# Experts of 704-column chunks: silu, product, turns and parts one to three units later, and a silu at the head of the loop

## The chip, the cores and the metric

The kernel runs on one core of a Trainium2 chip. The metric is the device time of one launch in microseconds (us). The kernel before takes 2733.32 us, the median of 3 runs (2729.62 to 2734.46).

## What is computed

Two groups of tokens (128 prompt, 512 sample; 640 together, model width 1024) go through a trunk of two layers. The second layer ends in a mixture of experts, and that stage is the one of this case. Its reference, cut to what matters:

```python
def swiglu(x, w_gu, w_dn):
    g, u = jnp.split(x @ w_gu, 2, axis=-1)
    return (jax.nn.silu(g) * u) @ w_dn

def moe_swiglu(h, router_w, router_b, w_gu, w_dn):
    ...
    _, idx = lax.top_k(logits + router_b.astype(jnp.float32), TOP_K)      # 2 of 8 experts
    ...
    for ex in range(N_EXPERTS):
        y = y + gates[:, ex:ex + 1] * swiglu(xf, w_gu[ex], w_dn[ex])      # 1024 -> 2 x 1408 -> 1024
```

## The kernel before

The expert stage is the loop of `tail_stage` over 17 tiles (`SLOT_TILES`) of 128 token slots each. A tile belongs to one expert. Every engine has its own loop over the tiles and, in it, its own row of 27 units (`NU`), written out by hand; semaphores tie the rows together.

- **Units.** A unit is one piece of weights. Units 0 to 3 are the gate weights of the first chunk of 704 columns (`ECH`), 4 to 7 its up weights, 8 to 11 and 12 to 15 the same for the second chunk (1408 columns to a partition each), and 16 to 26 are the eleven row blocks of the down weights (1024 columns to a partition each).
- **SyncE** (L3065 to L3076) loads unit u into a ring of 9 raw buffers, when VectorE has finished with unit u - 9.
- **ScalarE** (L3243 to L3266) copies unit u into `m_hi` (L3248, rounded to the fast float format), when TensorE has finished unit u - 9. Behind certain units it also does: the copy of the last tile's result (`AT_Y`, unit 4), the silu of a chunk's gates (`AT_SILU`, units 7 and 15), the high parts of the turned activations (`part_a`, `AT_PART_A`, units 14, 15, 21, 22), and the high parts of the next tile's turned rows (`part_x`, `AT_PART_X`, unit 19).
- **VectorE** (L3386 to L3400) makes `m_lo`, the rest of unit u (L3389), and behind certain units the product silu x up (`AT_ACT`, units 11 and 19, L3394), and the low parts belonging to the same `part_a` and `part_x` (L3378, L3373).
- **TensorE** (L3149 to L3196) multiplies unit u when `m_lo` of it is there: 12 matmuls of 352 columns for a gate or up unit (L3166 to L3169), 6 of 512 columns for a down unit (L3182 to L3186). Between units it transposes: `turn_a` c (L3134) turns part c of the 1408 activations, in the four parts of 2, 3, 3 and 3 blocks of 128 columns (`TA`), and `turn_x` (L3127) the rows gathered for the next tile (8 blocks, behind unit 16). The turns alternate between two banks of `p_turned`; a turn waits until VectorE has emptied its bank (L3138), and `turn_a` also for the product of its chunk (L3137).
- **Down units and parts.** Down unit k is unit 16 + k. Before k = 0, 2, 5 and 8 TensorE waits until VectorE has finished the low part of turn 0, 1, 2 or 3 (L3176 to L3178). So unit 21 (k = 5) waits for the parts of `turn_a` 2, and unit 24 (k = 8) for those of `turn_a` 3.
- **Other waits of TensorE.** Unit 8 waits for the first silu (L3156), unit 12 for the first product (L3159). Unit 0 of the next tile waits for the second silu and for the parts of the next rows (L3148).
- **Function tables.** ScalarE needs a table of functions in place. A load of one (ACT_TABLE_LOAD) is put in by the compiler ahead of an activation whose function is not in the table that it knows to be there. In this loop there is one ahead of the first copy of a tile (L3248) and one ahead of the first silu (L3261).

Of the kernel before, what the change touches and what calls it, by code (L numbers as in the profile page):

```python
# [18 lines left out]
ACT = mybir.ActivationFunctionType  # L19
# [6 lines left out]
P = 128  # L26
# [30 lines left out]
ECH = 2 * 352  # L57
# [2893 lines left out]
def tail_stage(K, z, flip, expert_of):  # L2951
# [9 lines left out]
    NTURN = len(TA) + 2  # L2961
    X_USES, A_USES = (2, 3), (0, 1, 4, 5)

    AT_Y, AT_SILU, AT_ACT, AT_PART_A, AT_PART_X = 4, (7, 15), (11, 19), (14, 15, 21, 22), 19
    assert NU % MRAW == 0 and NU % MSPLIT == 0
    ks = range(J // 2)
    tokens = [lambda j, t, h=h: h[:, j, t * P:(t + 1) * P] for h in (K.h_hi, K.h_lo)]
# [35 lines left out]
    with ExitStack() as ctx:  # L3003
        raw = K.sb(ctx, "m_raw", [P, MRAW, MUNIT])
        xg = K.sb(ctx, "x_gathered", [P, D])
        xh, xl = K.sb(ctx, "x_hi", [P, J, P], F32R), K.sb(ctx, "x_lo", [P, J, P], F32R)
        silu = K.sb(ctx, "m_silu", [P, ECH])
        act = K.sb(ctx, "m_act", [P, D_EXPERT])
        ah, al = K.sb(ctx, "m_a_hi", [P, DN, P], F32R), K.sb(ctx, "m_a_lo", [P, DN, P], F32R)
        ysb = K.sb(ctx, "y_slot", [P, D])  # L3010
        whi, wlo = K.sb(ctx, "m_hi", [P, MSPLIT, MUNIT], F32R), K.sb(ctx, "m_lo", [P, MSPLIT, MUNIT], F32R)
        idx = K.sb(ctx, "slot_tokens", [P, SLOT_TILES + 1], I32)

        K.sb(ctx, "gap", [P, 1000 - ECH // 2])
        tok, idx0 = K.sb(ctx, "token_ids", [P, NT], I32), K.sb(ctx, "first_tokens", [P, 1], I32)
        zero = K.sb(ctx, "slot_zero", [P, SLOTS // P], I32)
        pG, pU = K.ps(ctx, "p_gates", [P, 2, 512]), K.ps(ctx, "p_ups", [P, 2, 512])
        pT, pD = K.ps(ctx, "p_turned", [P, 2, 512]), K.ps(ctx, "p_down", [P, 2, 512])
        landed = [K.sig(f"m_landed{s}") for s in range(MRAW)]
        names = ("hi", "lo", "used", "silu", "act", "turned", "t_hi", "t_lo", "y")  # L3020
        s_hi, s_lo, s_used, s_silu, s_act, s_turned, s_thi, s_tlo, s_y = (K.sig("m_" + n) for n in names)
        s_clear = K.sig("m_cleared")
        s_stored, s_idx, s_gather = K.sig("m_stored"), K.sig("m_slots", own=True), K.sig("m_gathered", own=True)
        wgu = I["moe_w_gu"][0].rearrange("e (p j) (h n) -> e p j h n", j=J, h=2)
        wdn = I["moe_w_dn"][0].rearrange("e (j p) n -> e p j n", p=P)

        def gu(ring, u):
            return ring[:, u % ring.shape[1], :].rearrange("p (j q n) -> p j q n", j=2, q=2)

        def chunk_of(u):  # L3030
            c, r = divmod(u, 2 * KU)
            return c, *divmod(r, KU)

        def size(u):
            return MUNIT if u < GU else D


    def use(tile, j):
        return NTURN * tile + (2 + j)

    with nc.Block() as block:
# [38 lines left out]
        def _(pe):  # L3080
# [53 lines left out]
            def turn_a(tile, c):  # L3134
                a, b = TA[c]

                pe.wait_ge(s_act.sem, s_act.at(tile * CH + (c // 2 + 1)))  # L3137
                pe.wait_ge(s_tlo.sem, s_tlo.at(use(tile, A_USES[c]) - 1))  # L3138
                for j in range(a, b):
                    mm = pe.transpose(pT[:, A_USES[c] % 2, (j - a) * P:(j - a + 1) * P], act[:, j * P:(j + 1) * P], K.ident[:])  # L3140
                mm.then_inc(s_turned.sem, 1)
# [4 lines left out]
            with pe.Fori(0, SLOT_TILES) as tile:  # L3146

                pe.wait_ge(s_tlo.sem, s_tlo.at(NTURN * tile + 2))  # L3148
                for u in range(NU):  # L3149
                    s = u % MSPLIT  # L3150
                    if u < GU:
                        c, half, k = chunk_of(u)
                        acc = (pG, pU)[half]
                        if k == 0 and half == 0:

                            pe.wait_ge(s_silu.sem, s_silu.at(tile * CH + c))  # L3156
                        elif k == 0:

                            pe.wait_ge(s_act.sem, s_act.at(tile * CH + c))  # L3159
                        pe.wait_ge(s_lo.sem, s_lo.at(tile * NU + (u + 1)))  # L3160
                        h, l = gu(whi, u), gu(wlo, u)
                        for b in range(2):
                            j = 2 * k + b
                            start, stop = j == 0, j == J - 1
                            for q in range(2):
                                pe.matmul(acc[:, q, 0:ECH // 2], xh[:, j, :], h[:, b, q, :], start=start, stop=False)  # L3166
                                pe.matmul(acc[:, q, 0:ECH // 2], xh[:, j, :], l[:, b, q, :], start=False, stop=False)  # L3167
                            for q in range(2):
                                mm = pe.matmul(acc[:, q, 0:ECH // 2], xl[:, j, :], h[:, b, q, :], start=False, stop=stop)  # L3169
                        mm.then_inc(s_used.sem, 1)  # L3170
                    else:
                        k = u - GU
                        if k == 0:

                            pe.wait_ge(s_y.sem, s_y.at(tile + 1))
                        for c in range(len(TA)):  # L3176
                            if k == TA[c][0]:
                                pe.wait_ge(s_tlo.sem, s_tlo.at(use(tile, A_USES[c]) + 1))  # L3178
                        pe.wait_ge(s_lo.sem, s_lo.at(tile * NU + (u + 1)))
                        for half in range(2):  # L3180
                            cs = slice(half * 512, half * 512 + 512)
                            pe.matmul(pD[:, half, :], ah[:, k, :], whi[:, s, cs], start=k == 0, stop=False)  # L3182
                            pe.matmul(pD[:, half, :], ah[:, k, :], wlo[:, s, cs], start=False, stop=False)  # L3183
                        for half in range(2):
                            cs = slice(half * 512, half * 512 + 512)
                            mm = pe.matmul(pD[:, half, :], al[:, k, :], whi[:, s, cs], start=False, stop=k == DN - 1)  # L3186
                        mm.then_inc(s_used.sem, 1)
                    if u in (10, 11):
                        turn_a(tile, u - 10)
                    if u == 16:  # L3190

                        pe.wait_ge(s_gather.sem, s_gather.at(tile * 16 + 32))
                        for half in range(2):
                            turn_x(use(tile, X_USES[half]), half)
                    if u in (19, 20):
                        turn_a(tile, u - 17)  # L3196


        @block.scalar
        def _(a):  # L3200
# [39 lines left out]
                part_x(half, half, half)  # L3240
            a.wait_ge(s_clear.sem, s_clear.at(1))
            with a.Fori(0, SLOT_TILES) as tile:
                for u in range(NU):  # L3243
                    s = u % MRAW
                    a.wait_ge(landed[s].sem, landed[s].at((tile * (NU // MRAW) + (u // MRAW + 1)) * 32))

                    a.wait_ge(s_used.sem, s_used.at(tile * NU + (u - MSPLIT + 1)))
                    a.activation(whi[:, u % MSPLIT, 0:size(u)], raw[:, s, 0:size(u)], ACT.Copy).then_inc(s_hi.sem, 1)  # L3248
                    if u == AT_Y:

                        a.wait_ge(s_used.sem, s_used.at(tile * NU))
                        a.wait_ge(s_stored.sem, s_stored.at(tile * 16))
                        a.activation(ysb[:], pD[:].rearrange("p h n -> p (h n)"), ACT.Copy).then_inc(s_y.sem, 1)  # L3253
                        a.wait_ge(s_y.sem, s_y.at(tile + 1))
                        a.dma_start(K.y_slots[bass.ds(tile * P, P), :], ysb[:]).then_inc(s_stored.sem, 16)
                    if u in AT_SILU:
                        c = AT_SILU.index(u)
                        a.wait_ge(s_used.sem, s_used.at(tile * NU + (2 * KU * c + KU)))

                        a.wait_ge(s_act.sem, s_act.at(tile * CH + c))  # L3260
                        a.activation(silu[:].rearrange("p (q n) -> p q n", q=2), pG[:, :, 0:ECH // 2], ACT.Silu).then_inc(s_silu.sem, 1)  # L3261
                    if u in AT_PART_A:
                        part_a(tile, AT_PART_A.index(u))
                    if u == AT_PART_X:
                        for half in range(2):
                            part_x(use(tile, X_USES[half]), half, half)  # L3266
# [372 lines left out]
```

## Time and profile before

| what | value |
|---|---|
| median of 3 runs | 2733.32 us |
| the profiled execution: its time, its span | 2734.22 us, 2732.4 us |
| TensorE (PE) busy over the span | 2493.9 us, 91% |
| VectorE (DVE), ScalarE (ACT), GpSimd (POOL) busy | 59%, 51%, 15% |
| the expert loop, from the first weights copied to the last result | 1853 to 2688 us |
| time from one tile to the next in it | 48.74 us |

A matmul is pipelined, so the busy time of PE counts overlapping spans; what a unit costs is read as the distance from its first matmul to that of the next unit. PE stands for the matmuls and PEld for the weight loads of TensorE. In the timeline, neighbouring instructions of the same kind are merged to one row with their count, and square brackets hold the idle time of the engine ahead of the row and what ended it.

### The profile page before, as it was taken

The numbers are of one execution on the slowest core, as the hardware profiler recorded it, in microseconds if no ns is written. First come the engines' busy times: TensorE is split into PE (matmuls) and PEld (weight loads), VectorE is DVE, ScalarE is ACT, GpSimd is POOL, SyncE is SP. The second block draws the span as 40 slices with busy tenths as digits, with TensorE's granted clock in tenths as the row PEclk, the third lists the DMA queues.
The fourth block names the chain that finished last, engine by engine and source line by source line (L and its number), as shares of the span: only waits on it lengthen the run. The fifth ranks groups of instructions, "written<-read, shape, count | busy, mean of one in ns | idle before, by whom it ended". The sixth has DMA issues, their size and how long they took to land. (4 is left out here: it accounts for less than half of the span.)

```text
span 2732.4 us, 51986 instructions
## 1 busy us (share of the span) xinstructions
PE 2493.9 (91%) x19059; PEld 2159.2 (79%) x19059; DVE 1605.4 (59%) x2296; ACT 1386.4 (51%) x2083; POOL 397.5 (15%) x571
## 2 busy tenths in 40 slices
PE   6998969999789999899899788878999999999993
PEld 4887958778478888787677788767999989999892
DVE  3255566665753233223311688547888888888886
ACT  4235755554323333212222566417878788787883
POOL 1133122221141000011100343041000000000003
PEclk9999989999999999999899899978999999999997
DMA  7530000000541222223254000319999999999994
GB/s 270 202 126 3 18 5 3 3 3 3 205 147 47 77 77 69 77 77 127 98 191 145 31 19 10 119 69 356 382 370 380 383 367 384 368 378 386 366 386 188
DMA packets 193213, 472.23 MB, mean 173 GB/s; under 512 B 29436, under 2 KB 62844, under 8 KB 186916
## 3 DMA queue, kind: packets, MB, share of 16 engines
q1 hardware_dynamic: 185568, 445.69, 45.2%
q0 software_dynamic: 4416, 14.70, 1.5%
q10 hardware_dynamic: 3076, 9.71, 0.9%
q8 instruction: 108, 1.77, 0.3%
q14 instruction: 45, 0.37, 0.0%
HBM read 453.54 MB, written 16.48 MB: 172 GB/s over the span
## 5 line engine op out<-in xcount | busy, mean ns | idle before, releaser
L3389 DVE TENSOR_TENSOR m_lo<-m_raw,m_hi 128x1408 fp32r<-128x1408 f32 (+1 forms) x459 | 643.2, 1456 | 54.4 <-ACT m_hi L3248 49.3
L3248 ACT ACTIVATE m_hi<-m_raw 128x1408 fp32r<-128x1408 f32 (+1 forms) x459 | 537.5, 1241 | 15.5 <-ACT y_slot L3253 11.9
L213 PE MATMUL acc<-w_hi,h_hi 128*128 128x512 f32 (+1 forms) x1120 | 432.7, 386 | 17.2 <-PEq L2800 7.9
L195 DVE TENSOR_TENSOR w_lo<-w_raw,w_hi 128x1024 fp32r<-128x1024 f32 (+1 forms) x132 | 162.0, 1231 | 485.2 <-ACT w_hi L190 484.4
L214 PE MATMUL acc<-w_lo,h_hi 128*128 128x512 f32 (+1 forms) x1120 | 425.5, 380 | 0.0
L215 PE MATMUL acc<-w_hi,h_lo 128*128 128x512 f32 (+1 forms) x1120 | 425.5, 380 | 0.0
L190 ACT ACTIVATE w_hi<-w_raw 128x1024 fp32r<-128x1024 f32 (+1 forms) x134 | 135.1, 1012 | 456.8 <-PE acc L215 407.6
L213 PEld LDWEIGHTS acc<-w_hi,h_hi 128*128 128x128 f32 x1120 | 213.4, 191 | 79.7 <-issue 33.7
L215 PEld LDWEIGHTS acc<-w_hi,h_lo 128*128 128x128 f32 x1120 | 213.3, 190 | 34.6
L214 PEld LDWEIGHTS acc<-w_lo,h_hi 128*128 128x128 f32 x1120 | 213.7, 191 | 32.7
L3166 PE MATMUL p_gates<-m_hi,x_hi 128*128 128x352 f32 x544 | 179.3, 331 | 8.2 <-DVE m_lo L3389 8.2
L3167 PE MATMUL p_gates<-m_lo,x_hi 128*128 128x352 f32 x544 | 176.3, 325 | 0.0
L3166 PE MATMUL p_ups<-m_hi,x_hi 128*128 128x352 f32 x544 | 176.2, 325 | 0.0
L3167 PE MATMUL p_ups<-m_lo,x_hi 128*128 128x352 f32 x544 | 175.1, 323 | 0.0
L3182 PE MATMUL p_down<-m_hi,m_a_hi 128*128 128x512 f32 x374 | 152.7, 408 | 0.1
L3183 PE MATMUL p_down<-m_lo,m_a_hi 128*128 128x512 f32 x374 | 146.2, 391 | 0.0
L3169 PE MATMUL p_gates<-m_hi,x_lo 128*128 128x352 f32 x544 | 131.8, 323 | 0.0
L3169 PE MATMUL p_ups<-m_hi,x_lo 128*128 128x352 f32 x544 | 130.4, 320 | 0.0
L3422 POOL DMA_INDIRECT x_gathered<-scratch_h_rows,slot_tokens x17 | 17.0, 1002 | 743.7 <-PE p_turned L3131 737.1
L1232 POOL TENSOR_TENSOR x<-x,gated 128x512 f32<-128x512 f32 x30 | 46.9, 1586 | 535.2 <-DVE gated L1225 535.2
L3166 PEld LDWEIGHTS p_gates<-m_hi,x_hi 128*128 128x128 f32 x544 | 104.1, 191 | 15.3 <-DVE m_lo L3389 15.3
L3186 PE MATMUL p_down<-m_hi,m_a_lo 128*128 128x512 f32 x374 | 116.1, 392 | 0.0
(407 smaller groups left out, 4908.3 us busy)
## 6 DMA issues: line engine op xcount, KB each, us to landing
m_raw<-moe_w_gu SPq DMA_DIRECT2D x544, 352.0 KB
m_raw<-moe_w_dn SPq DMA_DIRECT2D x187, 512.0 KB
ada_w<-ada_w SPq DMA_DIRECT2D x40, 1024.0 KB, 4.9
w_raw<-ffn_w_gu SPq DMA_DIRECT2D x88, 256.0 KB, 2.9
w_raw<-w_in_o SPq DMA_DIRECT2D x24, 512.0 KB, 5.8
w_raw<-ffn_w_dn SPq DMA_DIRECT2D x22, 512.0 KB, 3.6
w_raw<-w_in_e SPq DMA_DIRECT2D x28, 384.0 KB, 5.2
scratch_y_slots<-y_slot ACTq DMA_DIRECT2D x18, 512.0 KB, 6.7
```

Source lines behind the costliest of these rows:

```text
L190: eng.activation(hi, self.raw_of(c, k), ACT.Copy).then_inc(self.hi.sem, 1)
L195: eng.tensor_tensor(lo, self.raw_of(c, k), hi, ALU.subtract).then_inc(self.lo.sem, 1)
L213: eng.matmul(out, hi, whi[:, b, :], start=first, stop=False)
L214: eng.matmul(out, hi, wlo[:, b, :], start=False, stop=False)
L215: mm = eng.matmul(out, lo, whi[:, b, :], start=False, stop=last)
L3166: pe.matmul(acc[:, q, 0:ECH // 2], xh[:, j, :], h[:, b, q, :], start=start, stop=False)
L3167: pe.matmul(acc[:, q, 0:ECH // 2], xh[:, j, :], l[:, b, q, :], start=False, stop=False)
L3169: mm = pe.matmul(acc[:, q, 0:ECH // 2], xl[:, j, :], h[:, b, q, :], start=False, stop=stop)
L3182: pe.matmul(pD[:, half, :], ah[:, k, :], whi[:, s, cs], start=k == 0, stop=False)
L3183: pe.matmul(pD[:, half, :], ah[:, k, :], wlo[:, s, cs], start=False, stop=False)
L3248: a.activation(whi[:, u % MSPLIT, 0:size(u)], raw[:, s, 0:size(u)], ACT.Copy).then_inc(s_hi.sem, 1)
L3389: dve.tensor_tensor(wlo[:, u % MSPLIT, 0:n], raw[:, u % MRAW, 0:n], whi[:, u % MSPLIT, 0:n], ALU.subtract).then_inc(s_lo.sem, 1)
```

## The change

Five things move, and one is added, all in the expert loop:

- the silu of a chunk's gates from behind units 7 and 15 to behind 8 and 16 (ScalarE);
- the product from behind units 11 and 19 to behind 13 and 21 (VectorE);
- `turn_a` 0 and 1 from behind units 10 and 11 to behind 12 and 13, and `turn_a` 2 and 3 from behind units 19 and 20 to both behind unit 20 (TensorE);
- the parts of the activations from behind units 14, 15, 21, 22 to behind 17, 18, 24, 25 (ScalarE and VectorE);
- the parts of the next rows from behind unit 19 to behind 22 (ScalarE and VectorE);
- a silu of one element per partition opens each pass of ScalarE's loop. Its result is not used. Its buffer is taken out of an unused gap, so that all others stay where they are.

```diff
-    AT_Y, AT_SILU, AT_ACT, AT_PART_A, AT_PART_X = 4, (7, 15), (11, 19), (14, 15, 21, 22), 19
+    AT_Y, AT_SILU, AT_ACT, AT_PART_A, AT_PART_X = 4, (8, 16), (13, 21), (17, 18, 24, 25), 22
...
-        K.sb(ctx, "gap", [P, 1000 - ECH // 2])
+        one = K.sb(ctx, "table_first", [P, 2])
+        K.sb(ctx, "gap", [P, 998 - ECH // 2])
...
-                    if u in (10, 11):
-                        turn_a(tile, u - 10)
+                    if u in (12, 13):
+                        turn_a(tile, u - 12)
...
-                    if u in (19, 20):
-                        turn_a(tile, u - 17)
+                    if u == 20:
+                        turn_a(tile, 2)
+                        turn_a(tile, 3)
...
             with a.Fori(0, SLOT_TILES) as tile:
+                a.activation(one[:, 1:2], K.ones[:, 0:1], ACT.Silu)
```

## Rows read from the trace of the kernel before

**Rows 1.** Busy time by stretch: us, PE, PEld, DVE, ACT, POOL (x), PEclk, DMA, GB/s.

```profile
2100.40:2149.10 48.70, 48.50 (x279) 44.92 (x278) 42.39 (x35) 38.74 (x39) 0.94 (x1) 1.00 0.99 377
```

**Rows 2.** Waits, 1850 to 2720 us: us in total, times, longest us.

```profile
PE p_gates L3166 <- DVE m_lo L3389: 8.2, 17, 5.0
...
PEld p_down L3182 <- DVE m_lo L3389: 7.5, 17, 0.5
...
ACT m_hi L3248 <- DMA m_raw<-moe_w_gu: 2.9, 3, 2.4
```

**Rows 3.** Timeline of PE, gate units: start us, us, instruction, count, idle before.

```profile
2202.18 0.32 PE L3166 MATMUL p_gates<-m_hi,x_hi 128*128 128x352 f32 x1
...
2204.10 0.32 PE L3166 MATMUL p_gates<-m_hi,x_hi 128*128 128x352 f32 x1
```

**Rows 4.** Timeline of PE, turns and down units, into the next tile.

```profile
2232.93 1.05 PE L3131 MATMUL p_turned<-ident,x_gathered 128*128 128x128 f32 x8
...
2237.94 0.49 PE L3140 MATMUL p_turned<-ident,m_act 128*128 128x128 f32 x3
...
2239.66 0.49 PE L3140 MATMUL p_turned<-ident,m_act 128*128 128x128 f32 x3
2239.90 0.48 PE L3182 MATMUL p_down<-m_hi,m_a_hi 128*128 128x512 f32 x1
...
2241.39 0.40 PE L3182 MATMUL p_down<-m_hi,m_a_hi 128*128 128x512 f32 x1
...
2244.44 0.39 PE L3182 MATMUL p_down<-m_hi,m_a_hi 128*128 128x512 f32 x1
...
2247.16 0.39 PE L3182 MATMUL p_down<-m_hi,m_a_hi 128*128 128x512 f32 x1
...
2248.87 0.43 PE L3166 MATMUL p_gates<-m_hi,x_hi 128*128 128x352 f32 x1 [0.19 <-DVE m_lo L3389]
...
2250.91 0.32 PE L3166 MATMUL p_gates<-m_hi,x_hi 128*128 128x352 f32 x1
```

**Rows 5.** Timeline of ACT, the same tile.

```profile
2209.04 1.28 ACT L3261 ACT_TABLE_LOAD   x1
...
2233.57 1.09 ACT L3232 ACTIVATE x_hi<-p_turned 128x512 fp32r<-128x512 f32 x2 [4.83 <-PE p_turned L3131]
...
2238.46 0.49 ACT L3237 ACTIVATE m_a_hi<-p_turned 128x384 fp32r<-128x384 f32 x1 [1.92 <-PE p_turned L3140]
2238.85 1.05 ACT L3248 ACTIVATE m_hi<-m_raw 128x1024 fp32r<-128x1024 f32 x1
...
2240.57 3.89 ACT L3248 ACTIVATE m_hi<-m_raw 128x1024 fp32r<-128x1024 f32 x4
2244.48 1.28 ACT L3248 ACT_TABLE_LOAD   x1
2245.78 6.45 ACT L3248 ACTIVATE m_hi<-m_raw 128x1408 fp32r<-128x1408 f32 x5
```

**Rows 6.** Timeline of DVE, the same tile.

```profile
2238.99 0.56 DVE L3378 TENSOR_TENSOR m_a_lo<-p_turned,m_a_hi 128x384 fp32r<-128x384 f32 x1 [0.99 <-ACT m_a_hi L3237]
...
2247.19 6.23 DVE L3389 TENSOR_TENSOR m_lo<-m_raw,m_hi 128x1408 fp32r<-128x1408 f32 x4 [0.90 <-ACT m_hi L3248]
```

**Rows 7.** Groups, 850 to 1150 us: busy us, mean ns | idle before, releaser.

```profile
L213 PE MATMUL acc<-w_hi,h_hi 128*128 128x512 f32 x398 | 155.7, 391 | 0.0
...
L190 ACT ACT_TABLE_LOAD x9 | 11.5, 1283 | 0.2
```

**Rows 8.** Timeline of ACT ahead of the loop: a small activation.

```profile
1841.27 0.21 ACT L3228 ACTIVATE choice_logits<-choice_logits 128x10 f32<-128x10 f32 x1 [15.04 <-DVE choice_logits L3361]
```

**Rows 9.** Stretches at 130 and 712 us, columns as in rows 1.

```profile
130.00:230.00 100.00, 93.45 (x594) 83.06 (x592) 52.65 (x69) 29.89 (x60) 31.51 (x22) 1.00 0.30 101
...
712.00:715.40 3.40, 3.18 (x9) 1.74 (x8) 0.82 (x1) 1.94 (x3) 1.21 (x1) 0.50 1.01 419
```

**Rows 10.** Waits of PE, 130 to 230 us.

```profile
PE shift_bank L988 <- ACT x L1042: 5.3, 4, 1.3
```

## The prediction

> **What bounds the kernel now.** I read the busy time by stretch first, then the waits of the expert loop, then the timelines of one tile, engine by engine. In a stretch as long as one tile TensorE is busy for 48.50 of 48.70 us at a granted clock of 1.00, while ScalarE has 10 us and VectorE 6 us of idle time [rows 1]. So TensorE sets the pace, and the other two and the loads have only to be in time. The loads are: DMA is at 377 GB/s with a share of 0.99 [rows 1], but ScalarE waited for a landing three times, 2.9 us in all [rows 2]. They have little to spare, and the change moves no more bytes.
>
> What TensorE loses is small. A gate or up unit takes 1.92 us from its first matmul to the next unit's [rows 3], a down unit 1.36 us (two of them 2.72, from 2244.44 to 2247.16) [rows 4]. All that is more than that in a tile is turns, a slower start behind each of them, and two waits for VectorE's low parts. One is at the head of the tile: in all 17 tiles the first gate unit waited for `m_lo`, 8.2 us in total, 5.0 of it once, so 0.2 us each in the others [rows 2]. The other is within the down units (7.5 us in 17 waits of the weight loads, 0.44 each) [rows 2]: units 22 and 23 took 3.05 us instead of 2.72 [rows 4]. Both come from the same thing. ScalarE is bound to TensorE's turns: the part of turn 2 stands behind its copy of unit 21, that of turn 3 behind 22, and it idles for 1.92 us until TensorE is done with unit 19 and turns [rows 5]. From there it has only a few copies' lead, and a table load of 1.28 us lies ahead of the next tile's first copy [rows 5].
>
> **The change, part by part.** I count from the end of unit 19, where turn 2 begins before (2237.94) [rows 4].
>
> *The head of the tile: a gain.* From the first matmul of unit 26 (2247.16) to that of unit 0 (2248.87) are 1.71 us, and from there to unit 1 (2250.91) 2.04 us [rows 4]. Undisturbed they are 1.36 and 1.92. So 0.35 + 0.12 = 0.47 us per tile can go, in 16 passages. Does the jump of the loop itself cost TensorE something? In the feed-forward loop, which passes its head nine times in a stretch (ScalarE's nine table loads there), TensorE's idle time is 0.0 [rows 7]; so I take nothing, with 0.1 us per passage as the other bound.
>
> *Turn 2 behind unit 20: a loss.* Before, turn 2 had unit 20 between itself and unit 21, which needs its parts. The path is: first transpose 2237.94, ScalarE's part starts at 2238.46 (0.52 later) [rows 4, 5], VectorE's low part at 2238.99 (0.53 later) and lasts 0.56 [rows 6]. It ended at 2239.55, and unit 21 began at 2239.90: covered by 0.35 us. After the change nothing stands between: unit 20, turn 2, turn 3, unit 21. The three transposes of turn 3 cover only their own length. From the first transpose to unit 21 I get 0.52 + 0.53 + 0.56 + 0.05 for the release = 1.66 us, where the two turns alone would take 0.49. That is a new wait of about 1.2 us in each tile, and all of TensorE's later work is queued behind it.
>
> The sum from the end of unit 19 to the start of unit 26: before 9.22 us (2237.94 to 2247.16) [rows 4]. After: unit 20 1.36 (no turn ahead of it now), the path 1.66, the slow start of unit 21 0.13 (it took 1.49, 2239.90 to 2241.39 [rows 4]), units 21 to 25 6.80: 9.95 us. So +0.73 us in each of 17 tiles. The gain of the wait at unit 23 and of one break less is already in it.
>
> *Are ScalarE and VectorE there when turn 2 is done?* It begins at 2239.30 on the clock of that tile (2237.94 + 1.36). ScalarE must be through copy 24: it idled 4.83 us ahead of the parts of the next rows [rows 5], and the three copies 20 to 22, at 0.97 us (3.89 for four [rows 5]), fit there; behind these parts (2234.66) copies 23 and 24 end by 2236.6. VectorE has the product and three low parts more ahead of the next rows' parts, by my count until 2236.5, and is through low part 24 by 2238.8; it is needed at 2240.4. So the 1.66 us stand alone.
>
> *Is the wait at the head really gone?* From turn 2's start: ScalarE's part begins at 0.52 and takes 0.39 (2238.46 to 2238.85 [rows 5]), copy 25 ends at 1.9, the part of turn 3 at 2.3, copy 26 at 3.2, table load and small silu at 4.7, copy 0 at 6.1 (6.45 for five [rows 5]), VectorE's low part 0 (6.23 for four [rows 6]) at 7.7. TensorE comes to unit 0 at 1.66 + 0.13 + 6 x 1.36 = 9.95. Spare: 2.2 us. Unit 23's low part was done before the turn.
>
> *The table load and the small silu.* Loads stand ahead of the first copy and of the first silu [rows 5], 1.28 us each. A silu at the head brings silu's table, and copies run on it already (no load ahead of those behind the first silu), so one load per tile goes. The small silu costs some 0.2 us (0.21 for a 10-element activation [rows 8]). That is 1.1 us of ScalarE per tile, at no gain in time: the head has its 2.2 us without it. In the first tile TensorE does wait for ScalarE, and 0.2 us are added once. The Trainium skill (ScalarE: Activation LUTs, What ACT_TABLE_LOAD costs) puts a change of set at about 2.66 us, as a drain of 1.38 us is added to the load. Here the four copies end at 2244.46, the load starts at 2244.48 and the next copy at 2245.78 [rows 5], so the rows show no drain. By the page the spare time at the head would be 0.8 us instead of 2.2, and the sum the same.
>
> *The other moves, at nothing.* Silu behind copy 8: TensorE needs it for unit 8, whose low part VectorE makes at the same time and for longer (1.6 us against 0.8). Product behind low part 13: unit 12 waits for it, so VectorE must now be two low parts and a product ahead at unit 12. It comes to the gates with the 2.2 us from the head in hand, wins 0.36 us per unit on TensorE (1.56 against 1.92), and the load of 1.28 us ahead of the silu is gone: cover about 4 us for a product of 0.9. Turns 0 and 1 cost the same two breaks. Unit 16 needs the part of turn 0, now behind copy 17: turn 0 is done two units before. The ring of nine copies allows a lead of eight units and the moves need five. SyncE's loads are issued when low parts are done, for units 20 to 24 earlier than before; no landing gets later.
>
> **The sum:** 17 x 0.73 = 12.4, less 16 x 0.47 = 7.5, plus 0.2: +5.1 us. The profiled execution took 2734.22 us, so 2739.3. It lies 0.9 above the median of the runs, on which I put the same 5.1: 2738.4 us, or 0.19% more. A measurement of this kernel tells about 0.2% (5.5 us) from no change, so this lies just inside.
>
> **The rivals.**
> - *Slower beyond doubt: the head keeps its wait.* If ScalarE or VectorE comes to the head over 2.2 us later than counted (say VectorE is behind at turn 2, since its low part 24 has 1.6 us to spare), the loss stays and the gain doesn't come: 12.4 + 0.2 gives 2745.9. For it: VectorE is busy for 42.4 of 48.7 us [rows 1]. Against: the idle times above. 8%.
> - *Not slower: the path of turn 2 is shorter than I read.* Its place is unit 21. It breaks even at 1.38 us instead of 1.66; hidden wholly, it would give -0.43 us and -0.47 us per tile, about 2718. It would need ScalarE to be released sooner by transposes that follow. Against it: in the turn of the next rows four more transposes follow the first four (2232.93), and ScalarE starts 0.64 later (2233.57) [rows 4, 5], the same delay behind the last of four as in turn 2 behind the last of three. 4%.
> - *The clock falls.* A wait of 1.2 us in each tile might make the granted clock fall from 2.4 to 1.2 GHz. It was 0.50 for the 3.4 us from 712.0 [rows 9]; one such step per tile costs 1.7 us, 29 in all: 2767. The rule behind it is in the Trainium skill (TensorE: Matmul & The Clock Gate, HAM oscillation), that a loop with a wait in each pass can fall back each time. Against it: between 130 and 230 us TensorE waited 1.3 us four times, 5.3 in all [rows 10], and the clock stayed at 1.00 [rows 9]. 3%.
> - *The compiler keeps the load at the silu.* ScalarE then has 1.3 us less between units 7 and 8, of about 4 to spare: the time of the forecast.
>
> **How the numbers follow.** The forecast of 2738.4 has 85%, with its own range of 2735 to 2742: the runs of before lie 4.8 us apart, the head's jump may cost up to 1.6, and the path is read to 0.1 us per tile. The range of 2732 to 2746 takes in the first rival and leaves out 2718 and 2767. Slower by over 0.2% (above 2738.8): 0.42 of the forecast's 85%, and the first and third rival, 0.47. Faster by over 0.2%: 0.04. Within: 0.49.
>
> **What would show it.** In the profile after: a wait of PE at the down units for VectorE's `m_a_lo` (L3378), 17 times at about 1.2 us; no wait of `p_gates` for `m_lo` but in the first tile; none at `p_down` for `m_lo`; 48.98 us from tile to tile; one table load per tile instead of two; ScalarE idle ahead of the second silu instead of ahead of the next rows. It is wrong if the waits at unit 21 are over 1.4 or under 0.9 us, if unit 12 waits for the product, or if ScalarE begins to wait for landings.

## The result, and the profile after

The kernel after takes 2740.73 us, the median of 9 runs (2738.39 to 2742.32), beside 2733.79 for the kernel before in 9 runs on the same chip (2728.47 to 2736.43). The ratio is 1.0028, with a 95% interval of 1.0017 to 1.0038. So the change is a small loss of 0.28%, or 6.9 us, and it stands clear of the scatter. The profiled execution took 2741.29 us; its span is the first line of the page:

```profile
span 2739.5 us, 52003 instructions
...
PE 2489.6 (91%) x19059; PEld 2164.9 (79%) x19059; DVE 1604.1 (59%) x2296; ACT 1366.2 (50%) x2083; POOL 401.1 (15%) x571
```

Nothing in this table of busy times tells of a loss. ScalarE even fell from 51% to 50%, because it loads half as many tables. The loss is in the waits. Here they are for the kernel after, from 1850 us on (us in total, times, longest us), and they answer to [rows 2]:

```profile
ACT m_silu L3264 <- PE p_gates L3170: 72.7, 17, 4.8
...
PEld p_down L3183 <- issue: 19.6, 17, 1.2
PE p_down L3183 <- DVE m_a_lo L3381: 15.7, 17, 0.9
...
ACT m_hi L3251 <- DMA m_raw<-moe_w_gu: 8.2, 13, 2.9
...
PE p_gates L3167 <- issue: 5.1, 1, 5.1
```

The wait at the head of the tile is left in the first tile alone (5.1 us, once), and the one of the down units for `m_lo` is gone. In their place stands one wait for `m_a_lo` in each of the 17 tiles. The view puts the part after the last transpose down to it, 0.92 us each; the weight load ahead of that matmul stood still for 1.15 us (19.6 / 17), which is nearly the whole gap of 1.17 (1.74 less the 0.57 that six transposes take up to the next matmul, as seen below).

The timeline of PE in the kernel after, one tile and the start of the next (start us, us, instruction, count, idle before), answers to [rows 4]:

```profile
2242.45 0.82 PE L3141 MATMUL p_turned<-ident,m_act 128*128 128x128 f32 x6
...
2288.81 0.39 PE L3183 MATMUL p_down<-m_hi,m_a_hi 128*128 128x512 f32 x1
...
2290.17 0.39 PE L3183 MATMUL p_down<-m_hi,m_a_hi 128*128 128x512 f32 x1
...
2291.53 0.82 PE L3141 MATMUL p_turned<-ident,m_act 128*128 128x128 f32 x6
2293.27 0.49 PE L3183 MATMUL p_down<-m_hi,m_a_hi 128*128 128x512 f32 x1 [0.92 <-DVE m_a_lo L3381]
...
2294.75 0.39 PE L3183 MATMUL p_down<-m_hi,m_a_hi 128*128 128x512 f32 x1
...
2300.19 0.39 PE L3183 MATMUL p_down<-m_hi,m_a_hi 128*128 128x512 f32 x1
...
2301.55 0.32 PE L3167 MATMUL p_gates<-m_hi,x_hi 128*128 128x352 f32 x1
...
2303.47 0.32 PE L3167 MATMUL p_gates<-m_hi,x_hi 128*128 128x352 f32 x1
```

Read as distances from start to start. From turn to turn: 2291.53 - 2242.45 = 49.08 us, one tile (49.06 to 49.08 from the second tile on, 48.72 to 48.74 before). Unit 20 takes 1.36 (2290.17 to 2291.53). The turns and the wait take 1.74 (to 2293.27) and unit 21 takes 1.48. From there to unit 26 (2300.19) there are 5.44 us, four undisturbed units of 1.36. Then come 1.36 to the first gate unit and 1.92 to the second, where before there were 1.71 and 2.04 [rows 4].

Where the 7.1 us between the two profiled executions came from:

| stretch | before | after | difference |
|---|---|---|---|
| launch to the first matmul of the loop | 1856.17 | 1857.26 | +1.1 |
| that matmul to the last result copy (2687.31; 2694.29) | 831.14 | 837.03 | +5.9 |
| from there to the end of the span | 45.1 | 45.2 | +0.1 |

Within the loop, the stretch from the end of unit 19 to the start of unit 26 is 10.02 us (2290.17 to 2300.19) against 9.22 before, and the passage of the head is 0.35 + 0.12 shorter, 0.48 by the mean over the tiles. 17 x 0.81 - 16 x 0.48 = 6.1, and 5.9 were measured. Of the 1.1 us ahead of the loop, 0.1 is the small silu of the first pass; 1.0 is there already at the first turned rows, where the code is the same:

```profile
1850.16 1.97 PE L3132 MATMUL p_turned<-ident,x_gathered 128*128 128x128 f32 x8 [8.95 <-DMA x_gathered<-scratch_h_rows,first_tokens]
...
1857.26 0.66 PE L3167 MATMUL p_gates<-m_hi,x_hi 128*128 128x352 f32 x1 [5.13 <-issue]
```

Before, these turns started at 1849.17, after a wait of 8.59 us. I count that 1.0 as scatter between executions: the runs of before lie 8 us apart, and in the twelve traces of this case whose code is the same up to there, these turns start between 1844.0 and 1851.3 us.

### The profile page after: what moved, and what is told of

It reads as the page before. It is cut to its first block and busy times, and to the rows that moved or that the text cites. A ratio compares the mean times of both kernels' runs of the same rounds, so it can differ in the third digit from the quotient of the medians.

```text
span 2739.5 us, 52003 instructions
## 1 busy us (share of the span) xinstructions
PE 2489.6 (91%) x19059; PEld 2164.9 (79%) x19059; DVE 1604.1 (59%) x2296; ACT 1366.2 (50%) x2083; POOL 401.1 (15%) x571
## 5 line engine op out<-in xcount | busy, mean ns | idle before, releaser
L2443 ACT ACTIVATE a_power<-p_unit 128x256 f32<-128x256 f32 (+1 forms) x200 | 69.6, 361 | 90.1 <-PE p_unit L2321 85.0
```

## The experiments

**The question.** By my theory the kernel after holds two things of opposite sign. Later parts (and with them a later product) take two waits away, and turn 2 directly ahead of unit 21 puts a larger one in. The rivals are that the new silu and the missing table load do something of their own, that it is the pairing of the turns and not the place of turn 2 that costs, and that one of the moves taken for free has a price. In what follows "tile" is the distance from one turn to the same turn a tile later. From the second tile on, the tiles of one execution agree in it to 0.03 us or better, far closer than the totals do. The first tile is longer in all of them, by about 1.9 us or more: its units 0 and 1 run, in whole or in part, at a granted clock of 0.50 (3.7 us for unit 0 instead of 1.92).

### Turns 2 and 3 back at their places, all else as after

```diff
-                    if u == 20:
-                        turn_a(tile, 2)
-                        turn_a(tile, 3)
+                    if u in (19, 20):
+                        turn_a(tile, u - 17)
```

> The changed kernel with turns 2 and 3 back behind units 19 and 20, all else as changed. Theory (the loss is the bare path from turn 2 to unit 21, 1.74 us in the trace after): unit 20 covers the path again, unit 19 to 22 take 1.61 + 1.72 + 1.49 = 4.82 us instead of 5.94, so 47.93 us from tile to tile instead of 49.06, no wait of PE for m_a_lo, about 2741 - 17 x 1.13 = 2721.5 us, faster than before by 0.45%. Rival (the later parts behind units 24 and 25 are the cause, whatever the place of the turn): the wait at unit 21 stays, since ScalarE comes to the part of turn 2 only behind copy 24, and the tile stays near 49 us.

Measured: 2716.47 us beside 2733.81 for the kernel before, ratio 0.9949 (0.9931 to 0.9968). Turns of PE in it, one tile apart:

```profile
2227.75 0.49 PE L3141 MATMUL p_turned<-ident,m_act 128*128 128x128 f32 x3
...
2275.67 0.49 PE L3141 MATMUL p_turned<-ident,m_act 128*128 128x128 f32 x3
```

A tile is 47.92 us, 1.14 less than after and 0.82 less than before. TensorE waits for nothing any more but in the first tile. So the place of one turn is the whole loss, and the rest of the change is worth 0.5% (0.82 x 17 = 14 us of 2734). The medians lie 17 us apart. In the profiled executions, of 17.8 us, 4.5 are an earlier start of the loop (1851.67 instead of 1856.17), which is within its scatter. This version beats both kernels.

### Both turns one unit earlier

```diff
-                    if u == 20:
+                    if u == 19:
```

> The changed kernel with both turns 2 and 3 behind unit 19 instead of 20. Theory: unit 20 stands between the turns and unit 21, 0.50 + 0.12 + 1.36 = 1.98 us against a path of 1.74, so no wait, and one slow start less than with the turns apart: 47.82 us per tile, about 2719.5 us. Rival (one unit more of lead is asked of VectorE, which must have emptied both banks of the next rows at the end of unit 19): a wait of PE for x_lo shows at the turn, and the tile is longer than with the turns apart.

Measured: 2719.23 us, ratio 0.9955 (0.9938 to 0.9971).

```profile
2227.47 0.82 PE L3141 MATMUL p_turned<-ident,m_act 128*128 128x128 f32 x6
2228.04 0.48 PE L3183 MATMUL p_down<-m_hi,m_a_hi 128*128 128x512 f32 x1
...
2275.37 0.82 PE L3141 MATMUL p_turned<-ident,m_act 128*128 128x128 f32 x6
```

The pair as such is harmless: a tile is 47.90, and the wait for `x_lo` that the rival asked for isn't there. It is also not the saving of a break that I had put at 0.1 us: six transposes take 0.57 us (2227.47 to 2228.04), and only 0.02 is left of it. What costs in the kernel after is that no unit lies between turn 2 and unit 21.

### Turn 2 ahead of unit 21, turn 3 behind it

```diff
-                    if u == 20:
-                        turn_a(tile, 2)
-                        turn_a(tile, 3)
+                    if u in (20, 21):
+                        turn_a(tile, u - 18)
```

> The changed kernel with turn 3 one unit later, behind 21; turn 2 stays behind 20. Theory (turn 3 runs inside the wait for the parts of turn 2, and costs nothing there): it now costs its own 0.25 us and a slow start of 0.12, 49.06 + 0.37 = 49.43 us per tile, with a wait at unit 21 longer by 0.25. Rival (the transposes of turn 3 hold up the parts of turn 2, which explains the 1.74 us against the 1.66 of the prediction): the path is 1.66 and the tile 49.35.

Measured (one execution): 2741.17 us.

```profile
2238.89 0.49 PE L3141 MATMUL p_turned<-ident,m_act 128*128 128x128 f32 x3
...
2288.32 0.49 PE L3141 MATMUL p_turned<-ident,m_act 128*128 128x128 f32 x3
2290.06 0.49 PE L3183 MATMUL p_down<-m_hi,m_a_hi 128*128 128x512 f32 x1 [1.25 <-DVE m_a_lo L3380]
```

The path is 1.74 us (2288.32 to 2290.06) with turn 3 behind turn 2 or without it. Its length does not depend on turn 3: three transposes more hide in it, and without them the wait grows by their length (from 0.92 to 1.25). They are paid behind unit 21 instead, and the tile is 49.43, as expected.

### The pair behind unit 20 in the kernel before

```diff
-                    if u in (19, 20):
-                        turn_a(tile, u - 17)
+                    if u == 20:
+                        turn_a(tile, 2)
+                        turn_a(tile, 3)
```

> The kernel before with one thing of the change: turns 2 and 3 both behind unit 20. Theory: the bare path of 1.74 us from turn 2 to unit 21 is added, and as ScalarE still has four copies, a table load and copy 0 behind the parts, the waits at unit 23 and at the head stay: from the first transpose 10.43 us to unit 0, so 1.36 + 10.43 instead of 10.93, +0.86 us, 49.6 us per tile, about +14.6 us. Rival (the loss at unit 21 gives ScalarE time to catch up, so that the head's wait goes by itself): 49.1 us per tile.

Measured (one execution): 2747.55 us, and both kinds of wait stand together in its waits from 1850 to 2690 us (the last tile's wait for `m_a_lo` lies behind that):

```profile
PE p_down L3182 <- DVE m_a_lo L3379: 14.7, 16, 0.9
...
PEld p_down L3182 <- DVE m_lo L3390: 11.1, 32, 0.4
...
PEld p_gates L3166 <- DVE m_lo L3390: 5.4, 16, 0.4
```

A tile is 49.70 (49.6 expected). With the first experiment this closes a square: the turn's move costs 0.96 us without the others (48.74 to 49.70) and 1.14 with them (47.92 to 49.06), and the others gain 0.82 and 0.64. The terms nearly add up; what overlaps is 0.18 us per tile. The starts of the units, as means over 15 tiles, say where. From unit 26 to unit 0 it is 1.43 us here, against 1.72 in the kernel before: TensorE comes later to the head and waits 0.29 less there. Units 21 to 24 together take 0.12 more. So the rival had a part of it right: the new wait takes some of the head's wait away, but only 0.29 us.

### The small silu alone, and everything but the small silu

```diff
             with a.Fori(0, SLOT_TILES) as tile:
+                a.activation(one[:, 1:2], K.ones[:, 0:1], ACT.Silu)
```

> The kernel before with the small silu at the head of the loop alone; nothing moved. Theory (ScalarE is tied to the turns 2 and 3, so what it wins in the middle of the tile it loses idling for a turn, and at the head the small silu adds its 0.12 us to a chain that TensorE waits for): one table load per tile, 48.73 + 0.12 = 48.85 us per tile, +1.9 us. Rival (the load saved is what frees the head): the wait of p_gates for m_lo goes and the tile falls to 48.26.

> The changed kernel without the small silu at the head of the loop. Theory (ScalarE has 2.2 us to spare at the head, and 4 us before unit 12, so neither the load nor the silu is on the path): two table loads per tile again, 49.06 us from tile to tile as in the changed kernel within 0.02, and the time within noise of 2741. Rival (the load ahead of the first silu costs TensorE time, as the sequence of ScalarE is on its path): the tile grows by up to 1.1 us, to 50.2, and the time by up to 18 us.

Measured: the kernel before with the silu 2733.69 us, ratio 1.0002 (0.9992 to 1.0012), a tile of 48.82, 0.08 more, which over 17 tiles is less than the totals can tell. The kernel after without it 2740.21 us, ratio 1.002 (1.0008 to 1.0033), a tile of 49.06 to 49.08, as with it. The second load is back in it, 17 times 1.28 us (groups of ACT in the loop: busy us, mean ns, idle before):

```profile
L3263 ACT ACT_TABLE_LOAD x17 | 21.8, 1283 | 2.3 <-PE p_gates L3170 0.4
```

A load more or less moves nothing in the kernel after, since ScalarE idles behind it, ahead of the second silu: for 4.3 us with one load per tile (72.7 / 17), for 3.4 with two. In the kernel before the silu adds its 0.2 us at the very spot where ScalarE is late, the head of the tile, and the 0.08 are seen there in the wait of the first gate unit (0.30 us instead of the 0.19 of [rows 4]):

```profile
2251.40 0.43 PE L3167 MATMUL p_gates<-m_hi,x_hi 128*128 128x352 f32 x1 [0.30 <-DVE m_lo L3391]
```

### Only the later parts, in the kernel before

```diff
-    AT_Y, AT_SILU, AT_ACT, AT_PART_A, AT_PART_X = 4, (7, 15), (11, 19), (14, 15, 21, 22), 19
+    AT_Y, AT_SILU, AT_ACT, AT_PART_A, AT_PART_X = 4, (7, 15), (11, 19), (14, 15, 24, 25), 22
```

> The kernel before with one thing of the change: the parts of turns 2 and 3 behind units 24 and 25 and those of the next rows behind 22 (before 21, 22 and 19). Turns, silu, product, parts 0 and 1 stay; no small silu. Theory (the head's wait and that of unit 23 come from ScalarE being held for turns 2 and 3 with four copies still to do, so this move alone frees them): no wait of PE for m_lo but in the first tile, 47.92 us per tile as with the turns apart, about 2718 us. Rival (the gain needs the later silu and product, or the table load saved, since VectorE is then late at unit 12 or at the head): a wait stays and the tile is 48.3 us or more.

Measured: 2724.46 us, ratio 0.9967 (0.9956 to 0.9978), a tile of 48.20. That is neither theory's number: both waits are gone, but from unit 20 to unit 21, where turn 3 lies between, there are 1.99 us instead of 1.72. VectorE's timeline in it shows why (its columns are those of PE's):

```profile
2276.25 0.89 DVE L3394 TENSOR_TENSOR m_act<-m_silu,p_ups 128x704 f32<-128x704 f32 x1 [1.25 <-PE p_ups L3169]
...
2281.66 2.35 DVE L3389 TENSOR_TENSOR m_lo<-m_raw,m_hi 128x1024 fp32r<-128x1024 f32 x2
2283.93 0.55 DVE L3378 TENSOR_TENSOR m_a_lo<-p_turned,m_a_hi 128x384 fp32r<-128x384 f32 x1
```

The product still stands behind low part 19, and there VectorE, now further ahead, waits 1.25 us for TensorE's up units. It has lost its lead when the part of turn 2 is due. By the steps of the path it could start at 2283.42 (2282.37 + 0.53 + 0.52); VectorE is at two low parts from 2281.66 and starts it at 2283.93. It ends at 2284.48, and unit 21 begins at 2284.60 (rows of PE):

```profile
2282.37 0.49 PE L3140 MATMUL p_turned<-ident,m_act 128*128 128x128 f32 x3
...
2284.09 0.49 PE L3140 MATMUL p_turned<-ident,m_act 128*128 128x128 f32 x3
2284.60 0.49 PE L3182 MATMUL p_down<-m_hi,m_a_hi 128*128 128x512 f32 x1
```

### The later parts with the second product later

```diff
-    AT_Y, AT_SILU, AT_ACT, AT_PART_A, AT_PART_X = 4, (7, 15), (11, 19), (14, 15, 21, 22), 19
+    AT_Y, AT_SILU, AT_ACT, AT_PART_A, AT_PART_X = 4, (7, 15), (11, 21), (14, 15, 24, 25), 22
```

> The kernel before with two things of the change: the parts of turns 2, 3 and of the next rows as in the changed kernel (24, 25 and 22), and the second product behind low part 21 instead of 19. Theory (with the parts alone unit 21 began 0.27 us late, since VectorE idled for the product until TensorE was done with unit 15, and came to low part 24 late): no wait at unit 21, 47.92 us per tile, about 2719 us. Rival (the table load saved, or the first silu and product, are needed too): the tile stays over 48.1.

Measured: 2719.11 us, ratio 0.9946 (0.9928 to 0.9965). VectorE in it no longer idles ahead of the product, and waits for ScalarE when the part of turn 2 comes:

```profile
2275.37 0.88 DVE L3394 TENSOR_TENSOR m_act<-m_silu,p_ups 128x704 f32<-128x704 f32 x1
...
2281.60 0.56 DVE L3378 TENSOR_TENSOR m_a_lo<-p_turned,m_a_hi 128x384 fp32r<-128x384 f32 x1 [0.75 <-ACT m_a_hi L3237]
```

A tile is 47.92, as in the first experiment. So four numbers of one line carry the whole gain: the parts behind 24 and 25, the next rows behind 22, the product behind 21. The moves of the silu, of the first product, of turns 0 and 1 and of their parts, and the small silu bring nothing. Which of the places 24, 25 and 22 are needed was not tried apart.

### The order of two waits

```diff
+                        pe.wait_ge(s_lo.sem, s_lo.at(tile * NU + (u + 1)))
                         for c in range(len(TA)):
                             if k == TA[c][0]:
                                 pe.wait_ge(s_tlo.sem, s_tlo.at(use(tile, A_USES[c]) + 1))
-                        pe.wait_ge(s_lo.sem, s_lo.at(tile * NU + (u + 1)))
```

> The changed kernel with TensorE's two waits ahead of a down unit in the other order: first for the low part of the weights, then for the part of the turned activations, which is the later one. Nothing else differs. Theory (of two waits the first is an instruction of its own, and the release from it costs 0.13 us instead of the 0.05 of the last one): the path is 1.66 us, as predicted, and the tile 48.98 us. Rival (the 0.08 us lie in the path itself): 49.06.

Measured (one execution): 2738.17 us, and a tile of 49.00 instead of 49.06. The total alone would tell nothing; the tile and the path do. In the kernel after VectorE's part starts at 2292.58 and takes 0.56, and unit 21 begins at 2293.27, 0.13 behind its end. ScalarE's and VectorE's parts there:

```profile
2292.06 0.49 ACT L3239 ACTIVATE m_a_hi<-p_turned 128x384 fp32r<-128x384 f32 x1 [3.28 <-PE p_turned L3141]
```

```profile
2292.58 0.56 DVE L3381 TENSOR_TENSOR m_a_lo<-p_turned,m_a_hi 128x384 fp32r<-128x384 f32 x1 [2.08 <-ACT m_a_hi L3239]
```

With the waits in the other order the late one comes last, VectorE's part (2290.09 + 0.56) ends at 2290.65, and unit 21 follows 0.05 later; the path is 1.66 us. Both releases are the same in all 17 tiles of their traces, to 0.01 us (rows of PE):

```profile
2289.04 0.82 PE L3141 MATMUL p_turned<-ident,m_act 128*128 128x128 f32 x6
2290.70 0.50 PE L3183 MATMUL p_down<-m_hi,m_a_hi 128*128 128x512 f32 x1 [0.85 <-DVE m_a_lo L3381]
```

### The silu once, ahead of the loop

```diff
+            a.activation(one[:, 1:2], K.ones[:, 0:1], ACT.Silu)
             for half in range(2):
                 part_x(half, half, half)
...
             with a.Fori(0, SLOT_TILES) as tile:
-                a.activation(one[:, 1:2], K.ones[:, 0:1], ACT.Silu)
```

(This one, and the next, with turns 2 and 3 behind 19 and 20.)

> The changed kernel with turns 2 and 3 behind units 19 and 20, and the small silu once ahead of the loop instead of at the head of each pass, where ScalarE waits for the first rows anyway. Theory: the first tile begins 1.3 to 1.5 us earlier if the compiler then leaves the load at the head of the loop out, and 47.92 us per tile as with the small silu in the loop: about 2716. If it puts both loads back (head and silu), the first tile begins as before and the tile is the same 47.92, as ScalarE has the time. Rival: with two loads per tile ScalarE is late at 47.92 us, and the tile is longer by 0.1 to 1 us.

Measured: 2717.24 us, ratio 0.9938 (0.9922 to 0.9955), a tile of 47.92. ScalarE's tables in the loop and just ahead of it come down to one:

```profile
L3240 ACT ACT_TABLE_LOAD x1 | 1.3, 1283 | 0.0
```

No pass of the loop has a load any more, 34 fewer than in the kernel before, and the tile is the same to 0.01 us: 47.92 with no load, with 17 (the first experiment) and with 34 (the later parts and product). ScalarE was not late. TensorE's first wait shrank from 5.1 to 3.6 us, but the first tile was 52.1 us long instead of 50.9, with short waits for the product and the parts. So nothing is shown to be gained over the first experiment.

### Turns 0 and 1 as a pair behind unit 13

```diff
-                    if u in (12, 13):
-                        turn_a(tile, u - 12)
+                    if u == 13:
+                        turn_a(tile, 0)
+                        turn_a(tile, 1)
```

> The changed kernel with turns 2 and 3 behind 19 and 20, and turns 0 and 1 both behind unit 13. Theory (one break less of TensorE's row; the pair behind 19 saved 0.02 us): 47.90 us per tile. Rival (a slow start saved is worth its whole 0.09 us here): 47.83. Either way no new wait, as unit 16 needs their parts two units later.

Measured: 2725.07 us, ratio 0.9969 (0.9958 to 0.9981), a tile of 48.05. Both numbers of the expectation fell: 0.13 us more than with single turns, not less. ScalarE had to wait for turn 0 itself:

```profile
2274.19 0.39 ACT L3239 ACTIVATE m_a_hi<-p_turned 128x256 fp32r<-128x256 f32 x1 [2.29 <-PE p_turned L3141]
```

That took the lead of ScalarE and, behind it, of VectorE, and the part of turn 2 (a row of VectorE) came at once after a low part, too late: from unit 20 to 21 there were 1.84 us instead of 1.72.

```profile
2285.96 0.55 DVE L3381 TENSOR_TENSOR m_a_lo<-p_turned,m_a_hi 128x384 fp32r<-128x384 f32 x1
```

But 0.13 us in 16 tiles is 2 us, and this version's median lies 8.6 above that of the first experiment. In the profiled executions the difference is 9.9 us: 4.0 of it lie ahead of the loop, 4.0 in the first tile (54.85 us instead of 50.88), where ScalarE waited for landings and TensorE then for the first product, and 2.0 in the other tiles. Whether the pair has to do with the 4.0 of the first tile is not shown.

## Why the prediction was right, and where it was off

- **TensorE sets the pace, and only its waits count.** Right. A table load per tile more or less changed nothing; 1.74 us between turn and unit did.
- **Turn 2 behind unit 20 opens a bare path.** Right in place, count and kind: 17 waits at the down units for `m_a_lo`, and unit 21 starts 1.17 us later than the turns alone would let it, as forecast. That this number fits so well is luck: the path was 0.08 us longer than summed, and the six transposes took 0.57 us instead of the 0.49 put down for them. Only the path enters the time. The term was a little too small. The path was summed as 0.52 + 0.53 + 0.56 + 0.05 = 1.66. It measured 0.53 (2291.53 to 2292.06), 0.52, 0.56 and 0.13, together 1.74. The step that failed is the release. The sum gives no source for its 0.05 us. That is what the waits of the kernel before at the head and at unit 23 show, where the late semaphore is the last one tested; at unit 21 it is tested first, and another wait follows. Exchanging the two brought the release back to 0.05 and the path to the forecast 1.66.
- **+0.73 per tile.** It was 0.80 to 0.81, the 0.08 of the release and nothing else: unit 21 took 1.48 (1.49 predicted) and units 22 to 26 their 1.36. (A slip that moves nothing: by its own terms the change breaks even at a path of 1.36 us, not 1.38.)
- **-0.47 at the head.** Measured 0.48, with no cost of the loop's jump. The spare time there was enough: no wait in 16 tiles. The rival in which the head keeps its wait (2745.9) is out.
- **The head's wait and that at unit 23 have the cause I named,** the parts' place in ScalarE's row; only, the product's place belongs to it. I had the product down as a move at nothing. In the kernel after it is, but for the reason that it moved too: left at 19, in the kernel before with the later parts, it costs 0.28 us per tile (48.20 against 47.92), since VectorE idles at it and is late at the part of turn 2. The working had looked only at whether anyone waits for a later product, not at what an early one makes its own engine wait for.
- **The other moves at nothing.** Unit 12 waits for no product, and the silu at 8, the turns at 12 and 13 and their parts cost nothing. ScalarE idles 4.3 us per tile ahead of the second silu, as said; but it still idles ahead of the next rows too (32.0 us in all) and, more than I had said, for the turns (76.3 us in 49 waits).
- **The compiler puts one load at the head and none at the silu.** Right, 17 in place of 34, each 1.28 us with no drain ahead of it: a copy ends at 2245.74, the load starts at 2245.76 and ends at 2247.04, and the silu starts at 2247.06.

```profile
2244.68 1.06 ACT L3251 ACTIVATE m_hi<-m_raw 128x1024 fp32r<-128x1024 f32 x1
2245.76 1.28 ACT L3245 ACT_TABLE_LOAD   x1
2247.06 0.20 ACT L3245 ACTIVATE table_first<-ones 128x1 f32<-128x1 f32 x1
```

- **The clock.** It stayed at its higher level, 2.4 GHz, granted in full (1.00) over a tile with a wait in it; a stretch as long as one tile, columns as in [rows 1]:

```profile
2100.40:2149.40 49.00, 48.08 (x279) 45.11 (x278) 42.30 (x35) 37.50 (x39) 1.36 (x1) 1.00 1.00 375
```

  It is down where TensorE has had little to do for longer, in both kernels alike. Ahead of the loop TensorE waits for the first rows (8.6 us before, 8.95 after) and then for the first weights (5.0 and 5.1 us), and starts the loop at 0.50, the lower level, 1.2 GHz. In the kernel before (columns as above):

```profile
1850.00:1862.00 12.00, 6.96 (x26) 6.56 (x25) 8.89 (x7) 10.64 (x10) 3.95 (x5) 0.50 0.99 220
```

  The rival of 2767 is out. The one of the shorter path (2718) too: the wait is there, and longer than read. Run without that wait, the kernel takes 2716.5, which is where this rival had put it.
- **"Wrong if ScalarE begins to wait for landings".** It did a little, 13 times and 8.2 us instead of 3 times and 2.9 [rows 2]. It was the wrong alarm: no wait of TensorE followed, and the faster version (2716.47 us) has 27 such waits, 13.9 us in all.
- **The size.** Forecast +5.1 us, measured +6.9 in the medians and +7.1 in the profiled executions. Of the difference of 2.0, 1.4 is the release (17 x 0.08), 1.0 arose ahead of the loop in unchanged code (scatter of the one profiled execution), and some 0.4 go the other way: the head (16 x 0.01), the small silu (0.1 instead of 0.2) and rounding. The forecast put the result just inside the bound of 0.2%, and it lies outside, at 0.28%.

**Left open:** what makes the gather ahead of the loop come up to 7 us earlier or later from one execution to the next, and whether the waits of the first tile for the product and the parts, seen in some versions (2 us of it with the silu ahead of the loop, 4 with turns 0 and 1 as a pair), are scatter or belong to the version.

## What to carry to other kernels

Between a step that hands work to another engine and the step that needs the answer there must lie at least as much independent work as the round trip takes (here 1.74 us, against a unit of 1.36 and the turn itself); putting two hand-overs together is harmless as long as that work lies behind the first. In a row written by hand, look at each step from both sides: who waits for it if it is later, and what its own engine waits for if it is earlier. And take a change of many parts apart before keeping or dropping it: here four numbers gained 0.82 us per tile, one turn's place lost 1.14, and the sum looked like a failed idea.

## What the runs showed of the hardware

- Where two semaphore waits follow each other on TensorE, the order shows: the release costs 0.13 us if the late one is tested first and 0.05 if it is tested last, in each of 17 tiles (path 1.74 and 1.66 us).
- Six transposes in a row take 0.57 us from the first to the next matmul, three take 0.25 (2282.27 to 2282.52, in the version with the later parts and product); joining two turns saved 0.02 us, not the 0.1 expected of one restart less.
- With copies and silus alone in the loop, the compiler left the table loads out of it altogether once a silu stood ahead of it: 34 loads of 1.28 us went, and the tile was 47.92 us with 34, with 17 and with none.
